# A two-layer encoder trunk with experts: the norm's root multiplied in behind the projections, and row halves for the first and last expert

## The reference, cut to what matters

```python
h = rms_norm(x, attn_norm_w[l])            # x * rsqrt(mean(x*x) + eps) * w
proj = h @ w_in[l]                         # 1024 -> 2444 columns
a_q, a_k, a_v, b_z, b_xbc, b_dt, c_q, c_k, c_v = jnp.split(proj, offsets, axis=-1)
x = x + jnp.concatenate([windowed attention(a), SSD mixer(b), differential attention(c)]) @ w_out[l]
h = rms_norm(x, ffn_norm_w[l])
# one group of 4 by argmax, then 2 of its 8 experts by softmax, weights combine = gate * p / sum(p)
x = x + sum over experts e of (silu(h @ w_gate[e]) * (h @ w_up[e]) * weights[:, e]) @ w_down[e]
```

## Time and profile before

| | us |
|---|---|
| median of 3 runs | 1249.18 (1249.11 to 1250.32) |
| the profiled execution | 1250.82 |
| its span, first to last instruction | 1249.0 |
| PE busy | 957.4 (77%) |
| DVE busy | 397.6 (32%) |
| ACT busy | 187.2 (15%) |
| hidden's matmuls (L562), busy | 310.3 |
| idle of PE just before them | 193.1, of which 189.1 ended by a weight landing |
| HBM read | 433.65 MB, 348 GB/s over the span |

### The profile page before, as it was taken

The page is one execution under the profiler, slowest core; times in us unless marked ns, Lnnn a source line. Parts: engine busy times, 40 slices in busy tenths (PEclk is TensorE's granted clock), DMA queues, the critical chain, the costliest instruction groups (busy, mean ns, idle before and its releaser), DMA issues.

```text
span 1249.0 us, 26485 instructions
## 1 busy us (share of the span) xinstructions
PE 957.4 (77%) x11004; PEld 605.4 (48%) x11004; DVE 397.6 (32%) x1224; ACT 187.2 (15%) x528; POOL 8.8 (1%) x27
## 2 busy tenths in 40 slices
PE   6999979666668787796689999786666666666964
PEld 5767855333334453453377777443333333333432
DVE  4668453111112222131166684521111111111213
ACT  1245221000000100010013452110000000000001
POOL 2000000000000000000000000000000000000000
PEclk8999989888889998998799999898888888888978
DMA  9825159999999999899994243599999999999994
GB/s 342 336 99 203 68 187 426 425 425 426 427 426 425 426 425 425 344 426 425 412 400 164 102 169 122 209 425 427 426 425 428 426 427 426 425 426 425 426 426 184
DMA packets 45961, 436.62 MB, mean 350 GB/s; under 512 B 8064, under 2 KB 10112, under 8 KB 21248
## 3 DMA queue, kind: packets, MB, share of 16 engines
q1 hardware_dynamic: 45824, 434.72, 84.1%
HBM read 433.65 MB, written 1.05 MB: 348 GB/s over the span
## 4 chain that ended last, share of the span: by engine, by line
PE 42%; DMA 40%; DVE 9%; issue 5%; DVEq 2%; ACT 1%; ACTq 0%
DMA ring<-in_w_up 39%; PE ps L562 16%; PE ps L638 7%; PE ps L573 4%; PE ps L761 3%; PE ps L650 2%; PE ps L543 2%; PE ps L582 2%; PE ps L701 1%; DVEq L1085 1%; PE ps L740 1%; PE ps L723 1%; PE ps L655 1%; DVE nmx L1258 1%; PE ps L692 1%
## 5 line engine op out<-in xcount | busy, mean ns | idle before, releaser
L562 PE MATMUL ps<-ring,xg 128*32 128x256 f32 x4096 | 310.3, 469 | 193.1 <-DMA ring<-in_w_up 189.1
L562 PEld LDWEIGHTS ps<-ring,xg 128*32 128x32 f32 x4096 | 166.7, 134 | 320.7 <-issue 273.5
L1062 DVE SCALAR_TENSOR_TENSOR gu<-th,ps 128x128 f32<-128x128 f32 x72 | 20.7, 288 | 615.2 <-ACT th L872 615.2
L573 PE MATMUL ps<-ring,actT 128*32 128x256 f32 x2304 | 139.2, 382 | 15.7 <-issue 13.3
L573 PEld LDWEIGHTS ps<-ring,actT 128*32 128x32 f32 x2304 | 69.0, 109 | 76.8 <-DVE actT L1066 24.1
L638 PE MATMUL ps<-hT,ring 128*128 128x256 f32 x416 | 99.5, 400 | 2.6 <-DVE hT L1112 2.6
L872 ACT ACTIVATE th<-ps 128x128 f32<-128x128 f32 x72 | 20.0, 278 | 526.8 <-PE ps L562 526.8
L638 PEld LDWEIGHTS ps<-hT,ring 128*128 128x128 f32 x416 | 82.2, 201 | 17.3 <-issue 2.4
L582 PE MATMUL ps<-ysb,PwT 32*128 32x256 f32 x1024 | 73.3, 400 | 1.0 <-ACT ysb L876 1.0
L543 PE MATMUL ps<-xh,Pb 128*32 128x256 f32 x1024 | 69.3, 387 | 0.0
L761 PE MATMUL ps<-ring,hT 128*128 128x256 f32 x256 | 59.2, 390 | 1.4 <-ACT hT L984 1.4
(11 more groups left out here) (251 smaller groups left out, 775.4 us busy)
## 6 DMA issues: line engine op xcount, KB each, us to landing
ring<-in_w_gate SPq DMA_DIRECT2D x64, 2048.0 KB, 43.0
ring<-in_w_up SPq DMA_DIRECT2D x64, 2048.0 KB, 37.9
ring<-in_w_down SPq DMA_DIRECT2D x64, 2048.0 KB, 42.4
ring<-in_w_in SPq DMA_DIRECT2D x8, 2048.0 KB, 20.4
ring<-in_w_out SPq DMA_DIRECT2D x4, 2048.0 KB, 20.3
ring<-in_w_in SPq DMA_DIRECT2D x2, 1584.0 KB, 27.2
x<-in_x SPq DMA_DIRECT2D x1, 1024.0 KB, 5.1
out<-fin SPq DMA_DIRECT2D x2, 512.0 KB, 2.7
```

Source lines behind the costliest of these rows:

```text
L562: last = mm(b_gate[j * SLOTS:(j + 1) * SLOTS, 0:2 * GQ], tokens[:, k, :], ring[:, low:high + 1:high - low, o:o + GQ], start=(k == 0), stop ...
L573: last = mm(b_y[j * SLOTS:(j + 1) * SLOTS, 0:DQ], actT[:, c * SLOTS:(c + 1) * SLOTS], ring[:, slot, o:o + DQ], start=(c == 0), stop=(c == ...
```

## The change

- The projections run on raw transposed states: ACT copies the transposes to `hT` with the norm's weight as scale, and the root is multiplied in when the projections are read out: by a row (`root_row`) on DVE for `xbc`, `cq`, `aq`, `ak`, `ck`, per token as a scale for `vz` and `cv` (ACT) and `dt` (DVE). In layer 1, PE does the first projection ahead of `rs`.
- The second norm's squares are taken by blocks of 256 columns as `xc2` makes them: three by ACT (`sa`), the last by DVE (`sd`); `rs2` sums four partial sums.
- The choice is written with fewer instructions (`first_key` has two single-tile instructions and a maximum), the root's exp and the weights come behind `rank`, the first expert's weighted picks and `places` behind its first `hidden`.
- `ORDER` is rewritten (dt in third place among the projections, conv.0 behind xbc.2).
- For experts 0 and 31, gate and up are cut by rows instead: a piece `front` has rows 0 to 3 of each partition's 8 of both matrices, `back` the rest, each loaded by two DMAs of 1 MB. `hidden` waits for `front`, does its half, frees it (`front_mm`), and waits for `back`.

```diff
+EDGES = (0, NE - 1)
-           + [(part, e) for e in range(NE) for part in ("gate", "up", "down")])
+           + [(part, e) for e in range(NE) for part in (("front", "back", "down") if e in EDGES else ("gate", "up", "down"))])
...
-    sq xT.0 xT.1 xT.2 xT.3 rs par conv.0 xbc.0 xbc.1 silu.0 conv.1 ak conv.2 xbc.2 xbc.3 silu.1 silu.2 conv.3
-    xbc.4 aq.0 silu.3 xs.0 conv.4 dt aS.0 silu.4 dta aq.1 xs.1 cum cumT sc.0 aq.2 nm.0 cb.0 cb.1 sc.1 rows.0 pT.0
-    seg.0.0 seg.0.1 sc.2 nm.1 xdt row.0.0 row.0.1 aS.1 vz.0 sc.3 seg.1.0 y.0 seg.1.1 row.1.0 row.1.1 seg.2.0 lam
...
-    ycn cT outB.0 outB.1 outB.2 outB.3 xc2.0 xc2.1 xc2.2 xc2.3 fT.0 fT.1 fT.2 fT.3 sq2 rs2 lg seed route rank hot
-    ov xn2
+    sq xT.0 xT.1 xT.2 xT.3 rs xbc.0 xbc.1 par dt xbc.2 conv.0 conv.1 silu.0 silu.1 xbc.3
+    conv.2 aq.0 silu.2 conv.3 ak xbc.4 aS.0 conv.4 dta silu.3 aq.1 silu.4 xs.0 sc.0 aq.2 cum
+    cumT sc.1 xs.1 nm.0 sc.2 seg.0.0 seg.0.1 cb.0 aS.1 rows.0 xdt pT.0 row.0.0 nm.1 row.0.1 cb.1
+    seg.1.0 vz.0 nm.2 y.0 seg.1.1 row.1.0 row.1.1 sc.3 seg.2.0 rows.1 seg.2.1 row.2.0 zs.0 row.2.1 ck.0 pT.1
...
+    od.3 nm.9 outA.3 ycn cT outB.0 outB.1 outB.2 outB.3 xc2.0 sa.0 xc2.1 sa.1 xc2.2 sa.2 xc2.3
+    sd fT.0 fT.1 fT.2 fT.3 rs2 lg seed xn2 wt cnt rank ov route
...
+                    k0 = HALF * FF * (part == "back")
+                    for h, w in enumerate((w_gate, w_up)):
+                        src = w[li, n, :, :].rearrange("(p k) f -> p (k f)", k=KC)[:, k0:k0 + HALF * FF]
+                        sp_.dma_start(to[:, h * HALF * FF:(h + 1) * HALF * FF], src).then_inc(signal, 16)
...
+                elif part == "front":
+                    sp_.wait_ge(M["front_mm"], len(EDGES) * li + EDGES.index(n) + 1)
...
+                if e in EDGES:
+                    for half, part in enumerate(("front", "back")):
+                        slot, signal, count = chunk(li, part, e)
+                        both = ring[:, slot, :].rearrange("p (h n) -> p h n", h=2)
+                        pe.wait_ge(signal, count)
+                        for k in range(HALF):
+                            for j in range(NQ):
+                                o = k * FF + j * GQ
+                                last = mm(b_gate[j * SLOTS:(j + 1) * SLOTS, 0:2 * GQ], tokens[:, half * HALF + k, :],
+                                          both[:, :, o:o + GQ], start=(half + k == 0), stop=(half == 1 and k == HALF - 1))
+                        last.then_inc(S["hidden_mm" if half else "front_mm"], 1)
+                    return
...
+                steps = list(PE_STEPS)
+                if li > 0:
+                    at = steps.index(("rs",))
+                    steps[at:at + 2] = steps[at + 1], steps[at]
...
-                                pe.wait_ge(h_ready, li * KC + k + 1)
+                                pe.wait_ge(done["act"], nth(li, "act", ("xT", k // 2)))
...
+                    elif kind == "sa":
+                        j = s[1]
+                        cs = slice(j * DQ, (j + 1) * DQ)
+                        act.wait_ge(done["dve"], nth(li, "dve", ("xc2", j)))
+                        for t in range(TT):
+                            last = A(squares[:, t, cs], xh[:, t, cs], ACT.Square, accum_out=part[:, t, j:j + 1])
...
+                    elif kind == "xT":
+                        for a in range(2):
+                            k = 2 * s[1] + a
+                            last = A(hT[:, k, :], bank[:, a * SEQ:(a + 1) * SEQ], ACT.Copy, scale=colp[:, K_AN + k:K_AN + k + 1])
...
-                    elif kind == "xbc":
-                        last = v.tensor_copy(xpad[:, s[1], TAPS // 2:TAPS // 2 + SEQ], bank[:, 0:SEQ])
+                    elif kind in ("xbc", "cq", "aq", "ak", "ck"):
+                        dve.wait_ge(done["act"], nth(li, "act", ("rs",)))
...
+                        last = v.tensor_tensor(to, bank[:, 0:SEQ], root_row[:, :], ALU.mult)
...
+                        def first_key(vals, top, score, key, k):
+
+                            for t in range(TT):
+                                v.scalar_tensor_tensor(score[:, t, :], vals[:, t, :], top[:, t:t + 1], tie[:, 0:k], ALU.is_equal, ALU.mult)
+                            dve.drain()
+                            v.reduce_max(key, score, AX_X)
+                            dve.drain()
```

More of the change, by code:

```diff
@@ L106 @@
 ON_PE = {"xT", "rs", "xbc", "dt", "cq", "aq", "ak", "cum", "xs", "cb", "cumT", "rows", "aS", "cS", "y", "vz", "pT", "ck", "cv", "oa", "od",
-         "yT", "cT", "outA", "outB", "fT", "lg", "seed", "rank", "ov"}
-ON_DVE = {"xc2", "hot", "sq", "xT", "par", "lam", "dt", "dta", "conv", "silu", "cum", "xdt", "seg", "row", "sc", "nm", "y", "zs", "ybn", "ycn", "sq2", "rs2",
+         "yT", "cT", "outA", "outB", "fT", "lg", "seed", "cnt", "rank", "ov"}
+ON_DVE = {"xc2", "wt", "cnt", "sq", "xbc", "cq", "aq", "ak", "ck", "par", "lam", "dt", "dta", "conv", "silu", "cum", "xdt", "seg", "row", "sc", "nm", "y", "zs", "ybn", "ycn", "sd", "rs2",
           "lg", "route", "rank", "ov"}
-ON_ACT = {"sq", "rs", "par", "lam", "dta", "cumT", "silu", "row", "sc", "vz", "zs", "pT", "ck", "cv", "oa", "od", "yT", "cT", "cq",
-          "aq", "ak", "xs", "cb", "sq2", "xn2", "route"}
+ON_ACT = {"sq", "rs", "par", "lam", "dta", "cumT", "silu", "row", "sc", "vz", "zs", "pT", "cv", "oa", "od", "yT", "cT",
+          "xT", "xs", "cb", "sa", "xn2", "route"}
 def shared(step):
-    return step[0] in ("xbc", "fT")
+    return step[0] == "fT"
 def on(engine, step):
@@ L176 @@
 SLOT_OF, HELD_BY = place_chunks()
-USES = {c: 1 + sum(SLOT_OF[b] == SLOT_OF[c] for b in ALL[:i]) for i, c in enumerate(ALL)}
+TRANSFERS = {c: 2 if c[1] in ("front", "back") else 1 for c in ALL}
+USES = {c: TRANSFERS[c] + sum(TRANSFERS[b] for b in ALL[:i] if SLOT_OF[b] == SLOT_OF[c]) for i, c in enumerate(ALL)}
 def reader(step):
@@ L183, in reader @@
         return "act" if step[1] % 2 == 0 else "dve"
-    return "dve" if step[0] in ("xT", "dt", "cum", "sc", "y", "lg", "rank", "ov") else "act"
+    return "dve" if step[0] in ("xbc", "cq", "aq", "ak", "ck", "dt", "cum", "sc", "y", "lg", "cnt", "rank", "ov") else "act"
 PE_STEPS = list(COUNT["pe"])
@@ L456, in _ @@
                         load_router(0)
-                    if li + 1 < DEPTH and i == PLACE["gate", 0] + RING + LATE - 1:
+                    if li + 1 < DEPTH and i == PLACE["front", 0] + RING + LATE - 1:
                         sp_.wait_ge(done["dve"], nth(li, "dve", ("lg",)))
@@ L816, in _ @@
                     hidden(M, xg[e % 2], li, e)
+                    if e == 0:
+                        pe.wait_ge(M["prep_ready"], 2 * first + 2)
+                        places(M, Pw[0])
                     if e + 1 < NE:
@@ L935, in _ @@
                     elif kind == "vz":
-                        last = A(vz[:, s[1], :], bank[:, :], ACT.Copy)
+                        act.wait_ge(done["dve"], nth(li, "dve", ("sq",)))
+                        last = A(vz[:, s[1], :], bank[:, :], ACT.Copy, scale=root[:, TT + s[1]:TT + s[1] + 1])
                     elif kind == "cv":
-                        last = A(cv[:, :, :].rearrange("p t n -> p (t n)"), bank[:, :], ACT.Copy)
+                        act.wait_ge(done["dve"], nth(li, "dve", ("sq",)))
+                        for t in range(TT):
+                            last = A(cv[:, t, :], bank[:, t * C_H * C_V:(t + 1) * C_H * C_V], ACT.Copy, scale=root[:, TT + t:TT + t + 1])
                     elif kind == "zs":
@@ L998, in _ @@
                 first = li * NE
-                places_copy(M, PwT[0], first + 1)
                 act.wait_ge(done["dve"], nth(li, "dve", ("ov",)))
```

199 lines of the change are left out of this document (95 added, 104 removed).

## The result

The changed kernel takes 1243.17 us (median of 5 runs, 1240.51 to 1247.12), the kernel before beside it 1249.18 (1248.08 to 1253.25): ratio 0.9944, 95% interval 0.9921 to 0.9968. It gained 6 us where 20.8 were forecast, and lies above the predicted range. Its profiled execution took 1243.33 us with a span of 1241.6, 7.4 less than the span before (1249.0).

A forecast was written before the change was run, and what follows sets the result against it. Expert weights stream at full DMA rate except in two dense-stage hollows, where PE holds the ring's slots. Savings 6.15 + 6.75 + 3.1 + 2.0 + 3.15 - 0.4 = 20.75 us gave 1228.4 us, range 1219 to 1240.

The forecast's parts named there:

- squares and choice: Between outB's end and hidden: earlier root chain, shorter choice and less work behind it, 4.6 us saved per layer.
- halves: Front and back pieces: earlier weight issue at layer starts, 3.1 and 2.0 us saved at layer ends, less 0.4.
- Inside the dense stage: Both dense stages: value 0 per layer, bounds 5.5 us saved and 15.5 us lost.
- The walk through both queues: PE and DVE in the dense stage: delays covered, margins 1.3 at cum, 2.7 at cb.0, 0 at y.0.
- rival B: DVE becomes the dense stage's bound, conv.0's delay never caught up: full price 15.5 us per layer, 1259; chance 0.10.
- Start of the experts: From outB's end to the first weight issue: 6.15 us saved in layer 0, 6.75 in layer 1.
- the front half: First expert's hidden: slot free after half of 4.3 us, 2.15 earlier; bounds 0 and 2.15.
- Halves and end of layers: Last expert: only the back half follows the last landing, saving 3.1 and 2.0 us, less 0.4 for DMAs.
- Rival D: Smaller DMAs at layer ends carry fixed cost queueing doesn't hide, 2.6 us each: 1238.8; chance 0.05.
- the rule of "DMA: Bandwidth & Descriptors": About 2.0 us fixed per DMA; two more DMAs at each layer end would cost 4 us an end.
- Start of layer 1: xbc.0 starts at 630.0 instead of 633.76, not waiting for the root: 3.15 us saved, bounds 2.0 and 4.9.
- rival E: Clock stays high for xbc.0 (1.7 us), half of 5.5 us idle per layer removed: 1221; chance 0.11.

The follow-up runs named there:

- tail_only: The kernel before with the squares by block and the shorter choice alone, no projections of raw states, no halves: 1245.9 us, ratio 0.9968.
- no_projection: The kernel before in its dense stage, with the change's other parts (squares by block, shorter choice, front and back halves): 1237.6 us, ratio 0.9899.
- dt_back: The changed kernel with dt alone moved back to just ahead of aS.0: 1237.3 us, ratio 0.9896.
- evac_twice: dt_back with each evacuation with the root made twice on DVE, the first into a spare tile: 1243.2 us, ratio 0.9947.
- after_again: The changed kernel profiled and timed once more, nothing altered: 1242.7 us, ratio 0.9932.
- no_halves: dt_back with gate and up loaded whole for experts 0 and 31, as in the kernel before: 1245.4 us, ratio 0.9954.
- warm_one: dt_back with 2.25 us of unread matmuls behind the seeding in the choice of experts: 1236.9 us, ratio 0.9896.
- warm_plain: no_projection with the same unread matmuls behind the seeding as warm_one: 1239.1 us, ratio 0.9910.
- dt_third: The kernel before with dt alone moved forward to third among its projections: 1263.2 us, ratio 1.0106.
- ak_first: The changed kernel with ak's evacuation ahead of conv.3 in DVE's queue, dt still third: 1245.2 us, ratio 0.9957.
- act_evac: The changed kernel with cq, aq, ak and ck read out by ACT without the root: 1245.1 us, ratio 0.9948.

## Why the prediction was wrong

Four kernels in a row divide the measured change, and the forecast's terms stand beside them. The differences add up to -6.9 where -6.0 was measured, and by the intervals each time is good to 1.4 to 3.5 us:

| part | from, to | measured | forecast |
|---|---|---|---|
| squares and choice | before 1250.1, tail_only 1245.9 | -4.2 | -9.2 |
| halves | tail_only, no_projection 1237.6 | -8.3 | -8.4 |
| projections, without dt's new place | no_projection, dt_back 1237.3 | -0.3 | -3.15 |
| dt third | dt_back, after 1243.2 | +5.9 | 0 |

- **Inside the dense stage: value 0.** This is the step that failed. The walk through both queues had margins of 1.3, 2.7 and 0 and called it covered. It did see conv.0 come 10.4 us late; in the trace it came 14.0 late (34.82 against 20.85), since PE's xbc.2 and dt ran partly at the lower clock. With a margin of 0 at y.0, any slip counted, and y.0's matmul came 6.7 late. In place of 0 the two stages cost 7.5 and 6.4 us. Of that PE's added waits are 2.5 and 3.9, which is rival B's mechanism at a quarter of its 15.5 or less; 5.0 and 2.5 are busy time at the lower clock, for which the forecast had no term inside the stage, and what decides that clock stays open. And I took dt's earlier place as a gain for dta, and did not ask what its 3.64 us on PE had covered where it stood. That the moved work costs little was wrong: evac_twice prices it at 0.7 us for each on DVE.
- **Start of the experts.** The path was right: 17.1 us up to hidden in layer 0 (4.4 saved, forecast 4.6; in after_again, with the low stretch earlier, 18.1 in both layers), 1.8 from the selection to the gather (forecast 2.0), SP's small loads done before the slot was free. The size that failed is the front half, priced at half of the 4.3 us of the whole hidden before, 2.15, and found at 3.7 and 3.5. In layer 0 the low stretch lies at 173.2 to 180.1 in the kernel before, over the gather and the first 1.3 us of hidden, and at 180.0 to 186.8 in this one, over the whole front half. In tail_only, without halves, the same two sizes make up the shortfall: hidden began 7.6 us earlier in sum instead of 9.2, and took 3.0 longer.
- **Halves and end of layers.** Right in mechanism and size: down waits for its landing (0.48 <-DMA), and from the first weights to the last down pass of layer 0 dt_back takes 434.8 us where no_halves takes 438.0, 3.2 saved. Rival D's fixed cost does not show on queued transfers of 1 MB, and with it the rule of "DMA: Bandwidth & Descriptors" in the Trainium skill, Anatomy of one DMA. That page fits its 2.0 us on DMAs issued through GpSimd; these are issued by SP, which the prediction did not say.
- **Start of layer 1.** The start 1.1 us after the Square was right, and the clock stayed high for most of it (rival E's part: the first projection took 3.8 us, priced at 5.4), so 5.1 came there instead of 3.15. But it is bought with DVE's extra work in both dense stages, which takes most or all of it back (0.3 us left by dt_back against no_projection, 2.2 by warm_one against warm_plain).
- **The range** ended at 1240, because B's price was cut to a chance of 0.10 rather than to a part: a delay that is partly caught up had no case of its own, and it is what came. Neither had the lower clock inside the stage.

## What to carry to other kernels

When an order is changed, ask of each moved step what it covered where it stood, not only when its own result is needed; a piece of the busy engine's work that waits for nothing is worth most of its length at the place where the other engine is behind (in dt_third 3.0 of dt's 3.64 us came back as a wait at cum). A margin of zero in a walk through two queues is a cost, and deserves its own case with a middle price. Time saved ahead of a matmul by shortening an idle stretch can be partly paid back, when the stretch at the lower clock then falls on the matmul (7.6 us saved, 3.0 paid back in tail_only). And before a small change to an engine with branches is judged, look whether the rest of its program, far from the edit (here the expert stage), changed too.

## What was not expected of the hardware

- Fourteen matmuls of one column per layer cost 11.8 us, through one more wait of 6.8 us at an extra pass and a pause of 3.3 us inside another, far away. Both end a fixed time after an instruction packet starts (4.0 and 2.4 us). Why five of seven extra passes don't wait stays open.
- TensorE was at its lower level (0.50) through 26.4 to 33.0 us of after while it was busy all the time, 6.60 of 6.60 us; in after_again too, at the same place, and not in dt_third or dt_back, nor in ak_first and act_evac, whose matmuls there are the same. What decides it stays open.
- A wait of 1.48 us between a gather at the full clock and hidden (warm_one) was followed by the lower level, and so was one of 1.06 in dt_back; one of 1.52 in evac_twice was not.
